# Attention in a hybrid diffusion layer: reciprocals of the softmax sums spread over partitions by a DRAM round trip instead of by a matmul

## The reference

```python
# 12 query heads in 4 groups of 3 heads (Q_PER_KV), 4 key/value heads, head width 64
def gqa_block(qi, k_all, v_all):            # 128 queries, 1,280 keys (latent and context)
    s = jnp.einsum('bqkgd,bskd->bkgqs', qi, k_all).astype(jnp.float32) * (HEAD_DIM ** -0.5)
    p = jax.nn.softmax(s, axis=-1).astype(v_all.dtype)
    return jnp.einsum('bkgqs,bskd->bqkgd', p, v_all)

x = x + g1 * (jnp.concatenate([four_x, attn_x], axis=-1) @ w_out[l])
x = x + g2 * expert_choice_ffn(modulate(x, norm_ffn_g[l], sh2, sc2), ...)
```

## Time and profile before

| | |
|---|---|
| median of 3 runs | 1982.06 |
| lowest, highest | 1981.98, 1985.96 |
| span of the profiled execution, first to last instruction | 1980.8 |
| mean granted TensorE clock | 0.971 |
| TensorE busy in the span | 1846.7 (93%) |
| VectorE, ScalarE, GpSimd busy | 1589.9, 1297.2, 315.4 |

### The profile page before, as it was taken

How to read it: one execution, slowest core, us unless ns; L and a number is a source line. 1 busy time by engine, 2 the same in 40 slices (tenths; PEclk the granted TensorE clock), 3 DMA queues, 4 the chain that set the end, 5 groups by cost and what they waited for, 6 DMA issues and landing times.

```text
span 1980.8 us, 27893 instructions
## 1 busy us (share of the span) xinstructions
PE 1846.7 (93%) x8691; PEld 1455.5 (73%) x8691; DVE 1589.9 (80%) x1971; ACT 1297.2 (65%) x1921; POOL 315.4 (16%) x305
## 2 busy tenths in 40 slices
PE   6999789999999999459999999999999999999995
PEld 3777666766776676248888888888888888888884
DVE  5887567867776676569998999899989989998986
ACT  4444366866676676237777777777777777777774
POOL 0343231211111111221100110011101001110113
PEclk8999899999999999669999999999999999999998
DMA  9566470110111010359999999999999999999996
GB/s 373 159 175 176 129 211 23 61 64 15 49 64 45 29 53 32 138 191 410 386 378 400 384 383 369 402 388 374 389 393 385 375 385 397 381 373 400 381 371 252
DMA packets 108034, 512.28 MB, mean 259 GB/s; under 512 B 12064, under 2 KB 36040, under 8 KB 57296
## 3 DMA queue, kind: packets, MB, share of 16 engines
q1 hardware_dynamic: 101792, 489.11, 65.2%
q0 software_dynamic: 4752, 17.30, 3.3%
q10 hardware_dynamic: 1440, 5.24, 0.7%
HBM read 481.71 MB, written 27.28 MB: 257 GB/s over the span
## 4 chain that ended last, share of the span: by engine, by line
PE 55%; DVE 2%; DMA 0%; issue 0%; ACT 0%; POOL 0%; POOLq 0%
PE banks L1645 35%; PE banks L1670 18%; PE banks L1657 1%; PE banks L1626 1%; DVE topi L1507 1%; DVE top L1505 1%; DVE cand L1508 1%; DVE raw L1600 0%; DMA xe<-h_scratch,icol 0%; DMA out<-raw 0%; DVE ysc L1567 0%; DVE ysc L1607 0%; ACT d_hi L1470 0%; POOL out L1430 0%; DVE x_lo L1533 0%
## 5 line engine op out<-in xcount | busy, mean ns | idle before, releaser
L1539 DVE TENSOR_TENSOR w_lo<-raw,w_hi 128x2048 fp32r<-128x2048 f32 x252 | 565.9, 2287 | 72.2 <-ACT w_hi L1448 72.2
L1448 ACT ACTIVATE w_hi<-raw 128x2048 fp32r<-128x2048 f32 x256 | 470.5, 1920 | 9.6 <-DMA raw<-in_w_exp 9.6
L1645 PE MATMUL banks<-w_hi,x_hi 128*128 128x512 f32 x1024 | 405.5, 396 | 1.4 <-DVE x_lo L1533 1.4
L1645 PE MATMUL banks<-w_hi,x_lo 128*128 128x512 f32 x1024 | 400.1, 391 | 0.0
L1645 PE MATMUL banks<-w_lo,x_hi 128*128 128x512 f32 x1024 | 399.5, 390 | 0.0
L1547 DVE TENSOR_TENSOR d_lo<-raw,d_hi 128x1024 fp32r<-128x1024 f32 x256 | 296.3, 1218 | 1.5 <-ACT d_hi L1470 1.4
L1470 ACT ACTIVATE d_hi<-raw 128x1024 fp32r<-128x1024 f32 x256 | 258.1, 1061 | 47.2 <-DMA raw<-in_w_exp 33.2
L1005 ACT ACTIVATE pth<-banks 128x384 fp32r<-128x384 f32 x320 | 157.3, 492 | 121.8 <-PE banks L1208 114.9
L1072 DVE TENSOR_TENSOR ptl<-banks,pth 128x384 fp32r<-128x384 f32 x320 | 177.4, 554 | 63.9 <-ACT pth L1005 57.0
L1645 PEld LDWEIGHTS banks<-w_hi,x_lo 128*128 128x128 f32 x1024 | 192.7, 188 | 40.8
L1645 PEld LDWEIGHTS banks<-w_hi,x_hi 128*128 128x128 f32 x1024 | 193.0, 188 | 39.8 <-DVE x_lo L1533 1.8
(11 more groups left out here) (219 smaller groups left out, 2759.6 us busy)
## 6 DMA issues: line engine op xcount, KB each, us to landing
raw<-in_w_exp SPq DMA_DIRECT2D x384, 1024.0 KB, 7.9
a_ring<-in_w_mod SPq DMA_DIRECT2D x32, 512.0 KB, 5.2
qt<-q_scratch SPq DMA_DIRECT2D x64, 192.0 KB, 3.4
a_slot<-in_w_mod SPq DMA_DIRECT2D x8, 1024.0 KB, 13.8
a_w_raw<-in_w_in SPq DMA_DIRECT2D x3, 2048.0 KB, 29.3
q_scratch<-a_qst SPq DMA_DIRECT2D x16, 384.0 KB, 3.9
xr<-in_x SPq DMA_DIRECT2D x8, 512.0 KB, 4.3
acc_scratch<-x SPq DMA_DIRECT2D x8, 512.0 KB, 2.6
```

The costliest lines, as they stand in the source:

```text
L1448: act.activation(w_hi[which][c][:, :], raw[which][c][:, :], ACT.Copy).then_inc(s["hi_done"], 1)
L1539: dve.tensor_tensor(w_lo[which][c][:, :], raw[which][c][:, :], w_hi[which][c][:, :].bitcast(F32), ALU.subtract).then_inc(s["lo_done"], 1)
L1645: i = pe.matmul(psum[:, 2 * (j % 2) + which, :], x_[par][:, k, :], w_, start=(k == 0 and w_ is hi and x_ is x_hi), stop=(k == KD - 1 and x ...
```

## The change

The reciprocals of a group, 128 x 3, are stored to a DRAM scratch `r_d` in the order heads, queries. When this store has landed, the row of 384 is loaded into all 64 partitions of the half of `rbc` that the group uses. Both transfers are issued by SyncE in a new function `spread(t, g)`. GpSimd's product into `mix` waits for the load. The product L954, the matmul L1244 and the copy L1014 go, and with them four of the ten uses of bank `MB` in a step. `diag` is replaced by an unused buffer of the same size. The overwriting of `rden` now waits for the store of the tile before.

```diff
+            def spread(t, g):
+                G = NKV * t + g
+                h = slice((g % 2) * HD, (g % 2 + 1) * HD)
+                sp.wait_ge(s["rden_done"], G + 1)
+                sp.dma_start(r_d[g].rearrange("r p -> p r"), rden[:, REP * g:REP * (g + 1)], allow_slow_non_contiguous=True).then_inc(s["r_out"], 16)
+                sp.wait_ge(s["r_out"], 16 * (G + 1))
+                sp.dma_start(rbc[h, :], r_d[g].rearrange("r p -> (r p)").partition_broadcast(HD)).then_inc(s["r_in"], 16)
             def step(t, prev, cur):
                 if cur and prev:
                     queries(t)
...
                     sp.dma_start(xr[:, :], x_d[t - 1]).then_inc(s["x_in"], 16)
+                    spread(t - 1, 3)
+                if cur:
+                    spread(t, 0)
+                if prev:
                     sp.wait_ge(s["x2_done"], t * 2)
                     sp.dma_start(acc_d.rearrange("(t p) d -> t p d", p=P)[t - 1], x2[:, :]).then_inc(s["x2_out"], 16)
+                if cur:
+                    spread(t, 1)
+                if prev:
                     sp.wait_ge(s["h2b"], 2 * t)
                     sp.dma_start(h2_d.rearrange("(t p) d -> t p d", p=P)[t - 1], h2[:, :]).then_inc(s["h2_out"], 16)
+                if cur:
+                    spread(t, 2)
...
                         pool.wait_ge(s["osum_done"], G + 1)
-                        pool.wait_ge(s["misc_free"], misc(t, use[f"R{i}"]) + 1)
+                        pool.wait_ge(s["r_in"], 16 * (G + 1))
                         pool.tensor_tensor(mix[h, 3 * (g // 2):3 * (g // 2) + REP, :].rearrange("p r n -> p (r n)"),
                                            osum[h, :], rbc[h, :], ALU.mult).then_inc(s["mix_done"], 1)
...
-                        pool.tensor_tensor(diag[g % 2][:, :, :], ident[:, :].unsqueeze(1).broadcast_to([P, REP, P]),
-                                           rden[:, REP * g:REP * g + REP].unsqueeze(2).broadcast_to([P, REP, P]), ALU.mult).then_inc(s["diag_done"], 1)
...
-                        if c == 1 and i in fl:
-                            act.wait_ge(s["misc_mm"], misc(t, use[f"R{i}"]) + 1)
-                            after(act, s["mix_done"], 4 * t + fl[i])
-                            act.activation(rbc[:, :], psum[:, MB, 0:REP * P], ACT.Copy).then_inc(s["misc_free"], 1)
...
-                            dve.wait_ge(s["diag_done"], NKV * (tb - 1) + g + 1)
+                            dve.wait_ge(s["r_out"], 16 * (NKV * (tb - 1) + g + 1))
...
-                        if c == 0 and i in fl:
-                            G = 4 * t + fl[i]
-                            pe.wait_ge(s["diag_done"], G + 1)
-                            misc_free(f"R{i}")
-                            pe.matmul(psum[:, MB, 0:REP * P], ones[:, :], diag[fl[i] % 2][:, :, :].rearrange("p r n -> p (r n)"),
-                                      start=True, stop=True).then_inc(s["misc_mm"], 1)
```

More of the change, by code:

```diff
@@ L116, in build @@
     acc_d = dram("acc_scratch", [N, D], F32)
+    r_d = dram("r_scratch", [NKV, REP, P], F32)
     with ctx:
@@ L137, in build @@
         nc_phase_b(nc, ctx, sem, sb, a, K, psum, ident, ones, rows, aff, cand, eps_c, ks, vs, qt, spectra, from_a,
-                   q_d, mod_d, h2_d, acc_d, x_d)
+                   q_d, mod_d, h2_d, acc_d, r_d, x_d)
         K.close()
@@ L774, in nc_phase_b @@
 def nc_phase_b(nc, ctx, sem, sb, a, K, psum, ident, ones, rows, aff, cand, eps_c, ks, vs, qt, spectra, from_a,
-               q_d, mod_d, h2_d, acc_d, x_d):
+               q_d, mod_d, h2_d, acc_d, r_d, x_d):
     G1, SH2, SC2, G2 = range(4)
@@ L786, in nc_phase_b @@
     ptl = sb("ptl", [P, 4, REP * P], F32R, B)
-    diag = [sb(f"diag{i}", [P, REP, P], F32, B) for i in range(2)]
     rbc = sb("rbc", [P, REP * P], F32, B)
@@ L791, in nc_phase_b @@
     mix = sb("mix", [P, KD, P], F32, B)
+    sb("fourier_hold", [P, 2 * REP * P], F32, B)
     wrt = sb("wrt", [P, KD, E], F32, B)
@@ L808, in nc_phase_b @@
         "w_in", "s_done", "mn_done", "exp_done", "t_done", "hi_done", "lo_done", "pv_done", "osum_done",
-        "rden_done", "diag_done", "misc_mm", "misc_free", "oth_done", "mix_done", "ymix_done", "x_in",
+        "rden_done", "r_out", "r_in", "misc_mm", "misc_free", "oth_done", "mix_done", "ymix_done", "x_in",
         "x2_done", "ss_done", "rstd_done", "mean", "h2a", "h2b", "h2_out", "x2_out", "neg_done", "lexp",
@@ L818, in nc_phase_b @@
     PTB, OB, MB = 4, 6, 7
-    MISC0 = 2
+    USES = 6
     EARLY, LATE = (0, 1, 2, 6, 7), (3, 4, 5)
@@ L827, in misc @@
     def misc(t, j):
-        return j if isinstance(t, int) and t == 0 else MISC0 + 10 * (t - 1) + j
+        return USES * (t - 1) + j
     def schedule(eng_step, eng):
@@ L836, in schedule @@
         eng_step(TL, True, False)
[L838 to L851, removed]
+    use = {n: i for i, n in enumerate(("OP0", "OP1", "HT0", "HT1", "RT", "AF"))}
     def flushes(prev, cur):
@@ L921, in step @@
             def step(t, prev, cur):
-                use = use_numbers(prev, cur)
                 fl = flushes(prev, cur)
```

## The result

| | before | after |
|---|---|---|
| median of 4 runs each | 1982.02 | 2057.06 |
| lowest, highest | 1981.62, 1985.96 | 2056.64, 2061.61 |
| span of the profiled execution | 1980.8 | 2055.0 |
| mean granted TensorE clock | 0.971 | 0.957 |

The ratio of the times is 1.0372, 95% interval 1.0359 to 1.0384: 75.0 us slower by the medians, 74.2 by the two spans. The prediction was 1984.3 and its range ended at 1997.

The account below looks back on a forecast made before the run. The ScalarE-VectorE chain at each flush, not TensorE, was taken as the bound: nothing gained, 2.2 us lost to late query loads, 1982.1 + 2.2 = 1984.3 us. Range 1977 to 1997, the forecast's own 1983 to 1986.

Parts of the forecast that it names:

- The removed work: At the flushes, 32 matmuls (0.7 us each, 22.4 in all), 32 copies (15.6) and GpSimd's diag products: priced at nothing.
- the chain named as its cover: At each flush, ScalarE and VectorE from oth through pth, ptl, osum, minimum and next ptl hold the fourth transposes, hiding the matmul.
- The sign foretold for it: TensorE's wait for ptl before the transposes grows from 10.0 us to about 30 in its 28 places.
- one flush for all: The flush at 590.7 us, with 0.61 us of idle TensorE, was taken to stand for all 28 waits.
- The path through the queue: On SyncE, group 2's store and read precede the next tile's query loads: late in tiles 1 and 2, +2.2 us together.
- W + 4.8 us: Store landing, read issue and two query loads on SyncE, 7.6 us in sum, to fit the 7.9 left before the scores.
- W: Time for the reciprocals' store to land, 384 pieces of 4 bytes: taken as 2.6 + 0.2 = 2.8 us.
- the end drawn from above, 5.4: Upper bound for the store's landing, from query stores of 384 pieces of 1 KB: 5.4 us at most, giving +18.4.
- My third rival: The granted clock falls because TensorE idles more, at most a few us in the thin last tile: 1986 us, chance 0.03.
- the round trip of group 3: From group 3's reciprocal to the osum it must meet: 9.6 us available, about 5 needed, so it costs nothing.
- Rival 2: Query loads late in every tile because 4-byte pieces are slow to write: 1990 to 2001 us, chance 0.30.
- Rival 1: TensorE is the bound and regains 0.7 us per flush: 1959.7 us, or 1971 with half; chance of both 0.13.

Follow-up runs that it names:

- the fourth experiment: The kernel after with its scratch ordered queries, heads, so the store has 128 pieces of 12 bytes instead of 384 of 4: 1987.94 us against 1983.41, ratio 1.0022.
- The kernel with both repairs: The kernel after with the next tile's queries of groups 0 to 2 ahead of group 2's pair, and 12-byte store pieces: 1984.07 us against 1984.96, ratio 0.9997.
- The idle kernel: Computes nothing of the layer; SyncE issues single transfers, four times per form: the change's store landed in 8.8 us, the same pattern read back in 2.1.
- the kernel with the pair beside: The kernel before, matmul and copy kept, plus the store and load at the same queue places into an unread buffer: 2044.48 us against 1984.96, ratio 1.0301.
- The faster kernel: The kernel with both repairs, plus the second ptl ahead of the second chunk's minimum on VectorE at each flush: 1975.79 us, ratio 0.9951 to the kernel before.
- the two kernels with VectorE's new order: Second ptl ahead of the second chunk's minimum at each flush: in the kernel before 1983.1 us (ratio 0.9990), in the kernel with both repairs 1975.79 (0.9951).
- With the queries first: The kernel after with group 2's store and load moved behind the next tile's query loads of groups 0 to 2: 1993.63 us against 1983.41, ratio 1.0056.

## Why the prediction was wrong

**The removed work: right in value, wrong in place.** Its price of nothing held (1.0003), and the chain named as its cover, from `oth` to the fourth transposes, kept its length (3.53 us in both). The sign foretold for it did not come: the wait for `ptl` was to grow from 10 to 30 us. It grew by 2, and the scores' wait for exponentials by 17. I had followed TensorE from the matmul straight to the late transposes and passed over the scores between them, which wait for a bank that ScalarE frees. I had also taken one flush for all: in the next one the fourth transposes come 3.17 us behind `oth` and not 3.53, and the 28 waits of the earlier trace rows are 0.36 us on average, not 0.61.

**The path through the queue: right in form, short in one term.** W + 4.8 us had to fit into 7.9. In the fourth experiment, with W at 2.3 at the median, tiles 2 to 6 were on time, as the sum says, and tile 7 was 0.4 late with W at 3.2, where the sum gives at most 0.1. The kernel with both repairs doesn't test this, since its queries stand ahead of the pair. Tile 1 of the fourth experiment was late by 3.5 us with a W of 2.0, where the sum gives 1.0: its second query load took 6.1 us to land where I had 3.3.

**The step that failed is W**, "I take W = 2.8", and the end drawn from above, 5.4. It measured 8.5. Neither row from which I drew the bounds had the form of this store: the earlier trace rows has 384 pieces of 1 KB, and in the earlier trace rows the small pieces are those of a load. The idle kernel shows that reading such pieces takes 2.1 us and writing them 8.8, so the load had said nothing of the store, and the upper bound was none. The Trainium skill ("DMA: Bandwidth & Descriptors", "Rules for kernel authors") warns of one descriptor per element, and the sentence that I set beside the sum pointed the right way; here the warning is borne out by 8.8 us, but the number of elements does not explain it, since as many pieces of the same size set 64 bytes apart land in 1.7. Its section "Specifications", with read-modify-write under 512 bytes, would have both forms alike and has the same gap. The 2.0 us that the prediction takes from "Anatomy of one DMA" are given there for transfers that GpSimd issues; these are SyncE's.

**The size of the loss, term by term.** With W = 8.5 my sum gives 5 x 5.3 + 7.5 + 6.1 = 40 us. Three things that it had not priced make up the rest:
- The loads are slower: from the reciprocal's end (613.50 + 0.18) to the first scores of that tile it is 15.0 us and not 8.5 + 4.8 = 13.3. Of the 1.7, 1.2 is the landing of the second query load (4.5 for 3.3) and 0.4 lies between the read's issue and the first query load. Over seven tiles that is 12; 40 + 12 is the 52.4 of the wait.
- The clock: a mean of 0.50 to 0.64 over 4.3 us behind each of the seven waits. The length times what is missing to 1.00, added over the seven stretches, is 13.9 us, if all of it counts. My third rival, a lower clock, was tied to the wrong waits, and to a wrong reading: the tile of the earlier trace rows that ran at 1.00 has waits for `ptl` of 0.6 us at most, not of 1.3. The clock's cost comes with the second rival, and whoever prices a wait of 6 us must price it too. The Trainium skill ("TensorE: Matmul & The Clock Gate", "HAM oscillation — how this bites in real kernels") describes this pattern, a wait for a DMA and then work at half clock; the trace agrees, 6.87 us of idle TensorE and then 0.50.
- The product that waits: the output projection waits 8.6 us for `mix` where it waited 1.7, 6.9 more. I had set the round trip of group 3 against `osum` and found 9.6 us enough for 5. It takes 650.28 - 636.63 = 13.7 in this tile:

```profile
645.62 0.56 DVE L1070 TENSOR_TENSOR osum<-banks,oth 64x384 f32<-64x384 f32 x1
...
650.28 0.99 POOL L944 TENSOR_TENSOR mix<-osum,rbc 64x384 f32<-64x384 f32 x1 [15.66 <-DMA rbc<-r_scratch]
...
651.40 1.98 PE L1146 MATMUL banks<-wout,mix 128*128 128x512 f32 x4 [1.82 <-POOL mix L944]
```

52.4 + 13.9 + 6.9 = 73.2, against 74.2 between the spans. That it closes so well is partly luck. By the starts of the tiles, tiles 1 to 7 are longer than before by 16.7 us besides their waits for queries, not by 13.9 + 6.9 = 20.8; tile 0 is 3.2 longer besides its own, and 1.9 come before the attention starts (first scores at 251.64 for 249.74). 52.4 + 16.7 + 3.2 + 1.9 = 74.2. So the clock and the product cost some 4 us less than their prices. The clock alone can be read where no product waits, in the kernel with the pair beside: there tiles 1 to 6 are longer by the next tile's wait and 1.2 to 2.4 us, 1.8 on average.

**The rivals.** Rival 2, slow small pieces, was the case, at a W beyond its own bounds. Rival 1 is refuted for this kernel. The faster kernel shows that the removed work has a worth, 1983.1 to 1975.8 between the two kernels with VectorE's new order, but only with that order. Matmul, copy and `diag` went together in every run, so how much of the 7.3 us belongs to the matmul is not shown.

**What stays open.** Why a packed row of 4-byte values is slow to write, and why query loads land 1.3 us later here. It is not their place behind the load of the reciprocals: in the fourth experiment they stand behind the same load, 576.96 and 578.05, and land in 3.6 at the median for 4.6. With the queries first it is the same, 4.7 with the stores of 4-byte pieces and 3.4 with those of 12. So the longer landing goes with the form of the store; how, no run shows.

## What to carry to other kernels

Before a small store takes the place of a matmul, look for a store of its very form, or bound it by none: here 384 values of 4 bytes took 8.8 us to land, and the same values as 12-byte pieces 2.5. A round trip through DRAM on a queue that also feeds the bound engine costs what stands behind its wait, so order the queue by due time; moving one pair behind the query loads brought back 63 of 75 us. And a wait of several us on TensorE is to be priced with the stretch at half clock behind it, here 1.2 to 2.4 us for a wait of 6 to 7.

## What the runs showed that was not expected

- Values of 4 bytes written side by side from 128 partitions land in 8.1 us; 8 bytes apart in 2.8 to 4.2, 16 bytes apart in 1.4 to 2.0, 32 bytes apart in 1.4 to 1.5. Three and six such rows take hardly more than one (8.8, 9.9), and the same pattern is read in 2.1.
- A small store with a landing in 1.4 to 1.7 us on the SyncE queue, less than any transfer of the kernel before in the earlier trace rows.
- TensorE's clock had a mean of 0.50 to 0.64 over 4.3 us behind waits of some 7 us, and stood at 0.50 for 4.6 behind one of 3.5. Behind the latter the tile was 1.0 us longer, less than half of the stretch.
- Query loads landed in 4.6 us (median) beside stores of 4-byte pieces and in 3.6 beside stores of 12-byte pieces, at the same place of the queue.
